# A transformer block on one core: the sums of squares of all eight tiles on VectorE, and one matmul with ones in place of three (two)

## The chip, the cores and the metric

The kernel runs on one core of a Trainium2 chip. TensorE multiplies, VectorE (DVE), ScalarE (ACT) and GpSimd (POOL) do the elementwise work, SyncE (SP) issues the loads of the weights. The metric is the device time of one execution in microseconds, the median of the runs shown.

## The reference, cut to what matters

Four layers of a first model and one layer of a second work on x of 256 tokens by 1024 channels, in float32. Each layer is an attention or a mixer, a projection back to 1024, and a gated feed-forward block. Ahead of each of these stands an RMS norm over the 1024 channels of a token:

```
def rmsnorm(x, g):
    xf = x.astype(jnp.float32)
    y = xf * lax.rsqrt(jnp.mean(xf * xf, axis=-1, keepdims=True) + EPS)
    return (y * g.astype(jnp.float32)).astype(x.dtype)
...
        x = x + m @ w_o[layer]
        h = rmsnorm(x, ffn_norm[layer])
        x = x + conv_gated_ffn(h, ffn_w_up[layer], ffn_conv_w[layer], ffn_conv_b[layer], ffn_w_down[layer])
```

The change touches only how the sum of xf * xf over the channels is made.

## The kernel before

x lies in SBUF transposed: eight tiles of 128 channels (partitions) by 256 tokens. A sum over channels is so a sum of the eight squared tiles, and then a sum over the 128 partitions, which a matmul with a 128x128 matrix of ones does (`statistic`); its result stands on every partition, in the bank `ov`.

The weights come in chunks of 1 MB or more through a ring of three buffers. Each chunk is split in two parts that TensorE can take fast: ACT rounds it to `w_hi` (L322), DVE makes the rest `w_lo` (L805). The activations are split the same way, `h_hi` by ACT and `h_lo` by DVE or POOL. A product takes three matmuls: hi by hi, lo by hi, hi by lo. All order is written by hand: each engine has one program, a loop over the stages (attention "da", "sb", "sw", "mix"; projection "wo"; "up"; "down"; "gate"), and semaphores tie them. A stage takes its chunks in turn.

There are 13 norms, listed in `SUMS`: "x" at the start, "wo0" to "wo3", "down0" to "down3", "final", "wo4", "res_a" and "down4". For each, ACT squares the tiles into `sq` (`squares`, L352), DVE adds them into `acc` (`add_squares`, L842) and TensorE sums over the partitions (`statistic`, L1601 for `acc`, L1605 for squares that are not in `acc`). For "down" norms each tile is squared by itself, and DVE has added seven; for the others tiles 0 to 5 are squared two by two and added by DVE, and tiles 6 and 7 go to TensorE as they are. Then `rms` on ACT (L365 Ln, L366 Exp) makes `rstd` out of the sum, DVE's `normalise` makes the normed tiles (`hf`, the rows `tmp<-x,par,rstd` of L854), ACT rounds them (`h_hi`, L376), and DVE (even tiles, L850) and POOL (odd tiles, L1345) make `h_lo`.

The first chunk of the stage behind "wo0" to "wo3", "down0" to "down2", "final" and "res_a" does not wait for the norm. It multiplies x times its gain, without rstd ("raw" tiles: `raw_high` on ACT L380, `raw_low` on DVE L863 and on POOL L1357 and L1360), and its result is scaled by rstd afterwards (`scaled_first`, L870, or L1235). In `first_outputs` TensorE walks over the eight tiles k; for each tile it does six matmuls (L1529 with `h_hi`, L1538 with `h_lo`), and at one k it does the statistic of the norm:

```
if raw is not None and k == (1 if raw[0:2] in ("wo", "do") else 5):
    statistic(raw)
```

The second chunk of the stage needs the normed tiles, and the third chunk is the first that is a plain product (L1484 to L1486). DVE's order behind a projection is: adding the last tiles to x, raw tiles 6 and 7, the `w_lo` of the stage's second chunk, `normalise`, the `w_lo` of its third chunk. ACT's is: `rms`, the `w_hi` of the third chunk (L322), `split_h` (L376). Behind a down projection DVE's is: raw tile 7, `normalise`, the scaling of the first chunk's result, the `w_lo` of three chunks.

For "x", "down3", "wo4" and "down4" the statistic stands alone, and TensorE has nothing of the next stage before the norm.

Of the kernel before, what the change touches and what calls it, by code (L numbers as in the profile page):

```python
# [33 lines left out]
S = 256  # L34
QB = 128
D = 1024
DT = D // P
# [47 lines left out]
def build(nc, xT, w_std, w_down, w_gate, params, consts, lam, onehot, tables, pT, out):  # L85
    ctx = ExitStack()
    with ctx:
# [10 lines left out]
        x = sb("x", [P, DT, S])  # L98
# [151 lines left out]
        SUMS = {}  # L250
        added = parts = 0
        for name, singles in ([("x", False)]
                              + [(f"{k}{l}", k == "down") for l in range(4) for k in ("wo", "down")]
                              + [("final", False), ("wo4", False), ("res_a", False), ("down4", True)]):
            SUMS[name] = (added, parts, len(SUMS))
            added, parts = added + (7 if singles else 5), parts + (8 if singles else 5)

        def is_single(name):
            return name[0:4] == "down"
# [537 lines left out]
        def _(dve):  # L797
# [25 lines left out]
            def add_squares(name, j):  # L823

                n = sum_part(name, j)[2]
                total = acc[:, 0:S]
                dve.wait_ge(sq_ready, SUMS[name][1] + j + 1)
                if is_single(name):
                    terms = [(total, sq[:, n, 0:S])]
                    before = j  # L830
                else:
                    terms = [(total, sq[:, n, 0:S]), (total, sq[:, n, S:2 * S])]
                    before = max(2 * j - 1, 0)
                    if j == 0:
                        terms = [(sq[:, n, 0:S], sq[:, n, S:2 * S])]
                for k, (a, b) in enumerate(terms):
                    if SUMS[name][0] + before + k:
                        dve.wait_ge(acc_done, SUMS[name][0] + before + k)
                    if j == 0 and is_single(name):
                        dve.tensor_copy(total, b).then_inc(acc_done, 1)  # L840
                    else:
                        dve.tensor_tensor(total, a, b, ALU.add).then_inc(acc_done, 1)  # L842
# [133 lines left out]
            dve.memset(odd[:, 7:8], EPS).then_inc(dve_step, 1)  # L976
            steps[0] += 1
            wait_step()
            for j in range(3):
                add_squares("x", j)  # L980
            split_lo(0, 0, SIZES[0])

# [39 lines left out]
            def sum_behind(name, k):  # L1022

                for t in (k - 1, k) if k == DT - 1 else (k - 1,):
                    if t >= 0 and raw_engine(app, t):
                        raw_low(app, t)
                if k % 2 and k > 1:
                    add_squares(name, k // 2 - 1)

            half = s_half = d_half = ffn = app = 0  # L1030
            layer = 0
# [2 lines left out]
            for kind, c0, n in STAGES:  # L1034
# [127 lines left out]
                elif kind == "wo":  # L1162
# [26 lines left out]
                    added_to_x(4)  # L1189
                    if layer < 4:  # L1190
                        raw_low(app, 6)
                        raw_low(app, 7)
                        next_split(c0, 2)
                        normalise(app, SUMS[name][2])
                        next_split(c0, 3)
                    else:
                        dve.wait_ge(rstd_done, SUMS[name][2] + 1)
                        def behind(k):
                            sum_behind("res_a", k)
                            if k == DT // 2:  # L1200
                                next_split(c0, 2)

                        add_normed("mix_post", x_ready, behind)
                        normalise(app, SUMS["res_a"][2])
                        next_split(c0, 3)
# [69 lines left out]
                elif kind == "down":  # L1275
                    name = f"down{layer}"
                    for k in range(DT):
                        if layer < 4:
                            dve.wait_ge(used, c0 + k + 1)
                            dve.tensor_tensor(x[:, k, :], pj[slot_of(c0, k)][:, 0:S], x[:, k, :], ALU.add)\  # L1280
                               .then_inc(x_main, 1)
                            dve.wait_ge(x_main, layer * DT + k + 1)
                            dve.tensor_tensor(x[:, k, :], pj[slot_of(c0, k)][:, S:2 * S], x[:, k, :], ALU.add)\  # L1283
                               .then_inc(bank_free, 1)
                        if k < DT - 1:
                            add_squares(name, k)
                        if layer < 3 and raw_engine(app, k):
                            raw_low(app, k)
                        if k < DT - 1:
                            next_split(c0, k)  # L1290
# [186 lines left out]
        def _(pe):  # L1477
# [38 lines left out]
            def first_outputs(app, sums, shared=True, raw=None):  # L1516

                for k in range(DT):  # L1520
                    if raw is None:
                        pe.wait_ge(h_hi_done, app * DT + k + 1)
                    else:
                        pe.wait_ge(raw_hi, raw_count(app, k))
                    for n, (dst, operands) in enumerate(sums):
                        (wh, wl), (xh, xl), swap = operands(k)
                        for w in (wh, wl):
                            a, b = (xh, w) if swap else (w, xh)
                            pe.matmul(dst, a, b, start=k == 0 and w is wh and (n == 0 or not shared),  # L1529
                                      stop=False, skip_group_check=shared)  # L1530
                    if raw is None:
                        pe.wait_ge(h_lo_odd if k % 2 else h_lo_even, app * (DT // 2) + k // 2 + 1)
                    else:
                        pe.wait_ge(raw_lo[raw_engine(app, k)], raw_lo_count(app, k))
                    for n, (dst, operands) in enumerate(sums):
                        (wh, wl), (xh, xl), swap = operands(k)
                        a, b = (xl, wh) if swap else (wh, xl)
                        done = pe.matmul(dst, a, b, start=False, stop=k == DT - 1, skip_group_check=shared)  # L1538
                    if raw is not None and k < DT - 1:
                        done.then_inc(raw_used, 1)  # L1540
                    if raw is not None and k == (1 if raw[0:2] in ("wo", "do") else 5):
                        statistic(raw)
                return done

# [50 lines left out]

            def statistic(name):

                singles = is_single(name)
                added, parts, _ = SUMS[name]
                pe.wait_ge(acc_done, added + (7 if singles else 5))  # L1600
                pe.matmul(ov[:, 0:S], ones, acc[:, 0:S], start=True, stop=False)  # L1601
                for j in ((7,) if singles else (3, 4)):
                    _, (a, b), n = sum_part(name, j)
                    pe.wait_ge(sq_ready, parts + j + 1)
                    done = pe.matmul(ov[:, 0:S], ones, sq[:, n, a:b], start=False, stop=j in (7, 4))  # L1605
                done.then_inc(stat_done, 1)

            def scores(s_half, q_tile, k_tile):
# [529 lines left out]
```

## Time and profile before

| | |
|---|---|
| median of 3 runs | 1587.36 us (1586.63 to 1589.05) |
| the profiled execution | 1588.9 us, its span from the first to the last instruction 1587.3 us |
| mean granted TensorE clock | 0.986 of full speed |
| busy share of the span | PE 96%, weight loads 91%, DVE 66%, ACT 54%, POOL 20% |
| loads of weights | 1 MB (most), landing 4.9 us after their issue |

The profile lists busy time by engine and the chain of work that ended last. An instruction's row gives its start, its duration, its engine and line, what it writes and reads, and in brackets how long the engine sat idle before it and which instruction released it. TensorE's rows overlap: a matmul of 256 columns lasts 0.28 us, and the next starts 0.12 us later at full clock. A matmul in float32 (the ones by `acc` or `sq`) appears as two rows, since it is done in two passes.

### The profile page before, as it was taken

The numbers are of one execution on the slowest core, as the hardware profiler recorded it, in microseconds if no ns is written. First come the engines' busy times: TensorE is split into PE (matmuls) and PEld (weight loads), VectorE is DVE, ScalarE is ACT, GpSimd is POOL, SyncE is SP. The second block draws the span as 40 slices with busy tenths as digits, with TensorE's granted clock in tenths as the row PEclk, the third lists the DMA queues.
The fourth block names the chain that finished last, engine by engine and source line by source line (L and its number), as shares of the span: only waits on it lengthen the run. The fifth ranks groups of instructions, "written<-read, shape, count | busy, mean of one in ns | idle before, by whom it ended". The sixth has DMA issues, their size and how long they took to land.

```text
span 1587.3 us, 31012 instructions
## 1 busy us (share of the span) xinstructions
PE 1527.1 (96%) x11566; PEld 1438.0 (91%) x11566; DVE 1050.1 (66%) x1671; ACT 862.6 (54%) x1347; POOL 316.1 (20%) x474
## 2 busy tenths in 40 slices
PE   6999999999999999988999999999999898899998
PEld 5988999899989998878999889899998797899997
DVE  5667877563378775667877566688776655866545
ACT  4766555455565554555656356665554455544533
POOL 2102212212222112212222220032110361212100
PEclk9999999999999999999999999999999898899999
DMA  7543656353335564442656455436564353355550
GB/s 258 160 168 110 210 185 241 136 180 112 127 110 209 185 243 135 152 160 80 212 185 214 169 178 162 153 119 205 182 241 153 104 189 107 133 185 195 190 205 27
DMA packets 36666, 264.65 MB, mean 167 GB/s; under 512 B 4767, under 2 KB 4826, under 8 KB 7792
## 3 DMA queue, kind: packets, MB, share of 16 engines
q1 hardware_dynamic: 33552, 255.59, 46.4%
q0 software_dynamic: 3040, 8.05, 2.0%
q8 instruction: 49, 0.80, 0.2%
q14 instruction: 25, 0.20, 0.0%
HBM read 262.50 MB, written 1.12 MB: 166 GB/s over the span
## 4 chain that ended last, share of the span: by engine, by line
PE 81%; DVE 11%; ACT 5%; issue 2%; DMA 1%; SPq 0%; POOL 0%; ACTq 0%; DVEq 0%
PE bank L1484 20%; PE bank L1485 19%; PE bank L1486 19%; PE bank L1495 10%; PE bank L1494 6%; DVE w_lo L805 3%; DVE tmp L854 2%; PE bank L1529 1%; ACT tmp L396 1%; ACT w_hi L322 1%; DVE acc L842 1%; PE bank L1637 1%; DVE tmp L886 1%; DVE h_lo L850 1%; DVE w_lo L814 1%
## 5 line engine op out<-in xcount | busy, mean ns | idle before, releaser
L805 DVE TENSOR_TENSOR w_lo<-w_raw,w_hi 128x2048 fp32r<-128x2048 f32 (+2 forms) x220 | 543.2, 2472 | 222.9 <-ACT w_hi L322 222.8
L1484 PE MATMUL bank<-h_hi,w_hi 128*128 128x256 f32 x2032 | 579.3, 285 | 2.1 <-DVE w_lo L805 2.1
L1485 PE MATMUL bank<-h_lo,w_hi 128*128 128x256 f32 x2032 | 574.9, 283 | 0.0
L1486 PE MATMUL bank<-h_hi,w_lo 128*128 128x256 f32 x2032 | 574.9, 283 | 0.0
L322 ACT CAST w_hi<-w_raw 128x2048 fp32r<-128x2048 f32 (+2 forms) x220 | 445.3, 2025 | 5.6 <-DMA w_raw<-w_std 2.8
L1484 PEld LDWEIGHTS bank<-h_hi,w_hi 128*128 128x128 f32 x2032 | 389.5, 192 | 8.0 <-issue 4.1
L1485 PEld LDWEIGHTS bank<-h_lo,w_hi 128*128 128x128 f32 x2032 | 389.7, 192 | 0.1
L1486 PEld LDWEIGHTS bank<-h_hi,w_lo 128*128 128x128 f32 x2032 | 389.6, 192 | 0.0
L1495 PE MATMUL bank<-act_both,w_hi 128*128 128x512 f32 (+1 forms) x704 | 248.7, 394 | 0.0
L734 ACT ACTIVATE tmp<-bank,par 128x256 f32<-128x256 f32 x181 | 93.4, 561 | 227.5 <-PE bank L1486 226.9
L1243 DVE SCALAR_TENSOR_TENSOR tmp<-bank,par,tmp 128x255 f32<-128x255 f32 (+1 forms) x362 | 155.4, 477 | 84.8 <-ACT tmp L734 82.1
L1494 PE MATMUL bank<-act_both,w_lo 128*128 128x256 f32 (+1 forms) x704 | 203.6, 289 | 0.0
L1484 PE MATMUL bank<-act_both,w_hi 128*128 128x256 f32 x516 | 150.5, 292 | 6.9 <-DVE act_both L958 5.2
L1495 PEld LDWEIGHTS bank<-act_both,w_hi 128*128 128x128 f32 (+1 forms) x704 | 131.9, 187 | 27.7
L1485 PE MATMUL bank<-act_both,w_hi 128*128 128x256 f32 x516 | 146.4, 284 | 0.0
L1486 PE MATMUL bank<-act_both,w_lo 128*128 128x256 f32 x516 | 146.4, 284 | 0.0
L1494 PEld LDWEIGHTS bank<-act_both,w_lo 128*128 128x128 f32 (+1 forms) x704 | 132.7, 189 | 15.0 <-issue 15.0
L1455 POOL CAST act_both<-tmp 128x256 f32 x110 | 43.6, 397 | 480.9 <-DVE tmp L1260 370.9
L352 ACT ACTIVATE sq<-x 128x256 f32<-128x256 f32 (+1 forms) x67 | 31.9, 479 | 161.9 <-DVE x L1283 149.6
L1484 PEld LDWEIGHTS bank<-act_both,w_hi 128*128 128x128 f32 x516 | 99.3, 192 | 13.2 <-DVE act_both L958 7.1
L1357 POOL TENSOR_SCALAR proj<-x,par 128x256 f32<-128x256 f32 x35 | 44.4, 1270 | 331.1 <-ACT h_hi L380 331.1
L1529 PE MATMUL bank<-h_hi,w_hi 128*128 128x256 f32 x320 | 92.8, 309 | 13.8 <-ACT h_hi L376 8.3
(165 smaller groups left out, 2130.5 us busy)
## 6 DMA issues: line engine op xcount, KB each, us to landing
w_raw<-w_std SPq DMA_DIRECT2D x181, 1024.0 KB, 4.9
w_raw<-w_down SPq DMA_DIRECT2D x40, 1408.0 KB, 6.2
act_both<-vec_dram POOLq DMA_DIRECT2D x56, 128.0 KB, 3.4
w_raw<-w_gate SPq DMA_DIRECT2D x4, 1280.0 KB, 5.4
x<-xT SPq DMA_DIRECT2D x2, 512.0 KB, 4.9
out<-x SPq DMA_DIRECT2D x4, 256.0 KB, 2.2
par<-params SPq DMA_DIRECT2D x1, 499.0 KB, 9.4
cst<-consts SPq DMA_DIRECT2D x1, 256.0 KB, 5.8
```

Of the source, the lines that this page charges most:

```text
L322: act.copy(w_hi[:, slot, 0:width], w_raw[:, slot, 0:width]).then_inc(hi_ready, 1)
L734: act.activation(to[:, slot, :], source, ACT.Identity, bias=col(3), scale=col(2)).then_inc(conv_init, 1)
L805: dve.tensor_tensor(w_lo[:, slot, 0:width], w_raw[:, slot, 0:width], w_hi[:, slot, 0:width].bitcast(F32), ALU.subtract).then_inc(lo_ready, 1)
L1243: return dve.scalar_tensor_tensor(to[:, slot, lag:S], source(v)[:, 0:S - lag], par[:, bass.ds(at + (4 * v + 2 - lag), 1)], to[:, slot, lag:S],
L1357: pool.tensor_scalar(proj[:, k % 4, :], x[:, k, :], gain_of(app, k), None, ALU.mult)\
L1455: pool.tensor_copy(act_hi[:, bass.ds(j, 1), :].squeeze(1) if not isinstance(j, int) else act_hi[rows, j, :], cval[rows, slot, :]).then_inc ...
L1484: pe.matmul(dst, wh, xh, start=first, stop=False, skip_group_check=shared)
L1485: pe.matmul(dst, wh, xl, start=False, stop=False, skip_group_check=shared)
L1486: done = pe.matmul(dst, wl, xh, start=False, stop=last, skip_group_check=shared)
L1494: pe.matmul(bank[:, 0:S], wl, xh, start=start and k == 0, stop=False, skip_group_check=True)
L1495: done = pe.matmul(bank[:, :], wh, pair, start=False, stop=stop and k == len(weights) - 1, skip_group_check=True)
L1529: pe.matmul(dst, a, b, start=k == 0 and w is wh and (n == 0 or not shared), stop=False, skip_group_check=shared)
```

## The change

DVE now adds all eight squared tiles into `acc`, and `statistic` is one matmul of ones by `acc`. `add_squares` has two more calls for the norms that squared pairs, and one more for the down norms. In `first_outputs` the statistic now stands behind tile 3 where a down norm is made, and behind tile 6 for all others.

```diff
             SUMS[name] = (added, parts, len(SUMS))
-            added, parts = added + (7 if singles else 5), parts + (8 if singles else 5)
+            added, parts = added + (8 if singles else 7), parts + (8 if singles else 5)
...
                     if j == 0:
                         terms = [(sq[:, n, 0:S], sq[:, n, S:2 * S])]
+                    elif j >= 3:
+                        terms = [(total, sq[:, n, (j - 3) * S:(j - 2) * S])]
+                        before = j + 2
...
-            for j in range(3):
+            for j in range(5):
                 add_squares("x", j)
...
                 if k % 2 and k > 1:
                     add_squares(name, k // 2 - 1)
+                if k == DT - 1:
+                    add_squares(name, 3)
+                    add_squares(name, 4)
...
                     if layer < 4:
                         raw_low(app, 6)
+                        add_squares(name, 3)
                         raw_low(app, 7)
+                        add_squares(name, 4)
                         next_split(c0, 2)
                         normalise(app, SUMS[name][2])
                         next_split(c0, 3)
                     else:
+                        add_squares(name, 3)
+                        add_squares(name, 4)
                         dve.wait_ge(rstd_done, SUMS[name][2] + 1)
...
-                        if k < DT - 1:
-                            add_squares(name, k)
+                        add_squares(name, k)
...
-                    if raw is not None and k == (1 if raw[0:2] in ("wo", "do") else 5):
+                    if raw is not None and k == {"d": 3, "w": 6}.get(raw[0], 6):
                         statistic(raw)
...
-                singles = is_single(name)
-                added, parts, _ = SUMS[name]
-                pe.wait_ge(acc_done, added + (7 if singles else 5))
-                pe.matmul(ov[:, 0:S], ones, acc[:, 0:S], start=True, stop=False)
-                for j in ((7,) if singles else (3, 4)):
-                    _, (a, b), n = sum_part(name, j)
-                    pe.wait_ge(sq_ready, parts + j + 1)
-                    done = pe.matmul(ov[:, 0:S], ones, sq[:, n, a:b], start=False, stop=j in (7, 4))
+                if name == "x":
+                    pe.wait_ge(consts_in, 16)
+                pe.wait_ge(acc_done, SUMS[name][0] + (8 if is_single(name) else 7))
+                done = pe.matmul(ov[:, 0:S], ones, acc[:, 0:S], start=True, stop=True)
                 done.then_inc(stat_done, 1)
```

The lines of the changed kernel are numbered three and more higher. TensorE at the head of the first up stage (norm "wo0"), before; the rows are of tiles 1 and 2:

```order
L1529 MATMUL bank<-h_hi,w_lo 128x256
L1538 MATMUL bank<-h_lo,w_hi 128x256 [waits raw_lo1]
L1538 MATMUL bank<-h_lo,w_hi 128x256
L1601 MATMUL bank<-acc,cst 128x256 [waits acc_done]
L1605 MATMUL bank<-sq,cst 128x256 [waits sq_ready] x2
L1529 MATMUL bank<-h_hi,w_hi 128x256 [waits raw_hi]
L1529 MATMUL bank<-h_hi,w_lo 128x256
```

And of the change, the rows of tiles 6 and 7 and the first of the second chunk:

```order
L1547 MATMUL bank<-h_lo,w_hi 128x256 [waits raw_lo1]
L1547 MATMUL bank<-h_lo,w_hi 128x256
L1610 MATMUL bank<-acc,cst 128x256 [waits acc_done]
L1538 MATMUL bank<-h_hi,w_hi 128x256 [waits raw_hi]
L1538 MATMUL bank<-h_hi,w_lo 128x256
L1538 MATMUL bank<-h_hi,w_hi 128x256
L1538 MATMUL bank<-h_hi,w_lo 128x256
L1547 MATMUL bank<-h_lo,w_hi 128x256 [waits raw_lo1]
L1547 MATMUL bank<-h_lo,w_hi 128x256
L1538 MATMUL bank<-h_hi,w_hi 128x256 [waits h_hi_done,bank_free,lo_ready]
```

Two of three matmuls with ones are gone, and between the remaining one and the second chunk stand six matmuls (tile 7), where there were 36 (tiles 2 to 7).

VectorE at the end of the first projection ("wo0"), before, from the last two adds to x on:

```order
L1176 TENSOR_TENSOR x<-bank,x 128x256 [waits tile6_done]
L1176 TENSOR_TENSOR x<-bank,x 128x256 [waits used]
L863 SCALAR_TENSOR_TENSOR h_lo<-x,par,h_hi 128x256 [waits raw_hi] x2
L805 TENSOR_TENSOR w_lo<-w_raw,w_hi 128x2048 [waits hi_ready]
L854 SCALAR_TENSOR_TENSOR tmp<-x,par,rstd 128x256 [waits rstd_done]
L854 SCALAR_TENSOR_TENSOR tmp<-x,par,rstd 128x256 x3
L850 TENSOR_TENSOR h_lo<-tmp,h_hi 128x256 [waits h_hi_done]
```

And of the change:

```order
L1182 TENSOR_TENSOR x<-bank,x 128x256 [waits tile6_done]
L1182 TENSOR_TENSOR x<-bank,x 128x256 [waits used]
L866 SCALAR_TENSOR_TENSOR h_lo<-x,par,h_hi 128x256 [waits raw_hi]
L845 TENSOR_TENSOR acc<-acc,sq 128x256 [waits acc_done,sq_ready]
L866 SCALAR_TENSOR_TENSOR h_lo<-x,par,h_hi 128x256 [waits raw_hi]
L845 TENSOR_TENSOR acc<-acc,sq 128x256 [waits acc_done,sq_ready]
L805 TENSOR_TENSOR w_lo<-w_raw,w_hi 128x2048 [waits hi_ready]
L857 SCALAR_TENSOR_TENSOR tmp<-x,par,rstd 128x256 [waits rstd_done]
```

Two adds stand between the raw tiles and ahead of the `w_lo` of the second chunk.

VectorE at the end of the first down projection ("down0"), before:

```order
L1280 TENSOR_TENSOR x<-bank,x 128x256 [waits used]
L1283 TENSOR_TENSOR x<-bank,x 128x256 [waits x_main]
L863 SCALAR_TENSOR_TENSOR h_lo<-x,par,h_hi 128x256 [waits raw_hi]
L854 SCALAR_TENSOR_TENSOR tmp<-x,par,rstd 128x256 [waits rstd_done]
L854 SCALAR_TENSOR_TENSOR tmp<-x,par,rstd 128x256 x3
```

And of the change:

```order
L1290 TENSOR_TENSOR x<-bank,x 128x256 [waits used]
L1293 TENSOR_TENSOR x<-bank,x 128x256 [waits x_main]
L845 TENSOR_TENSOR acc<-acc,sq 128x256 [waits acc_done,sq_ready]
L866 SCALAR_TENSOR_TENSOR h_lo<-x,par,h_hi 128x256 [waits raw_hi]
L857 SCALAR_TENSOR_TENSOR tmp<-x,par,rstd 128x256 [waits rstd_done]
```

The eighth add stands ahead of the raw tile 7. The orders of ACT, POOL and SP are the same as before.

## Rows read from the trace of the kernel before

**Rows 1.** The page: busy time and share by engine, with the instructions' count.

```profile
PE 1527.1 (96%) x11566; PEld 1438.0 (91%) x11566; DVE 1050.1 (66%) x1671; ACT 862.6 (54%) x1347; POOL 316.1 (20%) x474
```

**Rows 2.** The page: shares of the chain that ended last.

```profile
PE 81%; DVE 11%; ACT 5%; issue 2%; DMA 1%; SPq 0%; POOL 0%; ACTq 0%; DVEq 0%
```

**Rows 3.** The lines of the statistic: duration min/median/max in ns, first and last start.

```profile
L1601 PE MATMUL bank<-acc,cst x26: 377/379/792, 8.7 to 1549.9; 128*128 128x256 f32 x26
L1605 PE MATMUL bank<-sq,cst x42: 378/379/634, 9.6 to 1550.6; 128*128 128x256 f32 x42
```

**Rows 4.** Timeline around norm "wo0", TensorE: start, duration, row, idle before and releaser.

```profile
137.89 0.70 PE L1601 MATMUL bank<-acc,cst 128*128 128x256 f32 x2 [0.90 <-DVE acc L842]
139.29 1.40 PE L1605 MATMUL bank<-sq,cst 128*128 128x256 f32 x4 [0.70 <-ACT sq L352]
140.34 0.47 PE L1529 MATMUL bank<-h_hi,w_hi 128*128 128x256 f32 x1
...
151.82 0.39 PE L1484 MATMUL bank<-h_hi,w_hi 128*128 128x256 f32 x1 [0.43 <-DVE w_lo L805]
```

**Rows 5.** Timeline around norm "wo0", VectorE.

```profile
139.66 0.48 DVE L863 SCALAR_TENSOR_TENSOR h_lo<-x,par,h_hi 128x256 fp32r<-128x256 f32 x1 [0.55 <-ACT h_hi L380]
140.37 0.48 DVE L863 SCALAR_TENSOR_TENSOR h_lo<-x,par,h_hi 128x256 fp32r<-128x256 f32 x1 [0.22 <-ACT h_hi L380]
140.77 2.29 DVE L805 TENSOR_TENSOR w_lo<-w_raw,w_hi 128x2048 fp32r<-128x2048 f32 x1
142.97 1.67 DVE L854 SCALAR_TENSOR_TENSOR tmp<-x,par,rstd 128x256 f32<-128x256 f32 x4
144.56 0.41 DVE L850 TENSOR_TENSOR h_lo<-tmp,h_hi 128x256 fp32r<-128x256 f32 x1
...
148.94 2.82 DVE L805 TENSOR_TENSOR w_lo<-w_raw,w_hi 128x2048 fp32r<-128x2048 f32 x1
```

**Rows 6.** Timeline around norm "wo0", ScalarE, and GpSimd's last raw tile.

```profile
140.73 0.47 ACT L365 ACTIVATE rstd<-bank,odd 128x256 f32<-128x256 f32 x1 [0.39 <-PE bank L1605]
141.56 1.90 ACT L322 CAST w_hi<-w_raw 128x2048 fp32r<-128x2048 f32 x1
...
138.71 0.72 POOL L1360 TENSOR_TENSOR h_lo<-proj,h_hi 128x256 fp32r<-128x256 f32 x1
```

**Rows 7.** Timeline around norm "down0", TensorE.

```profile
330.30 0.59 PE L1601 MATMUL bank<-acc,cst 128*128 128x256 f32 x2
330.73 0.59 PE L1605 MATMUL bank<-sq,cst 128*128 128x256 f32 x2
...
341.89 0.38 PE L1484 MATMUL bank<-w_hi,h_hi 128*128 128x256 f32 x1 [0.50 <-DVE w_lo L805]
```

**Rows 8.** Timeline around norm "down0", ScalarE and VectorE.

```profile
331.36 0.48 ACT L365 ACTIVATE rstd<-bank,odd 128x256 f32<-128x256 f32 x1 [0.74 <-PE bank L1605]
...
332.32 1.67 DVE L854 SCALAR_TENSOR_TENSOR tmp<-x,par,rstd 128x256 f32<-128x256 f32 x4 [1.18 <-ACT rstd L366]
...
339.56 6.70 DVE L805 TENSOR_TENSOR w_lo<-w_raw,w_hi 128x2048 fp32r<-128x2048 f32 x3
```

**Rows 9.** Timelines around norms "down3", "final" and "res_a".

```profile
1241.22 0.70 PE L1605 MATMUL bank<-sq,cst 128*128 128x256 f32 x2 [0.80 <-ACT sq L352]
...
1251.43 0.88 DVE L842 TENSOR_TENSOR acc<-acc,sq 128x256 f32<-128x256 f32 x2
...
1357.67 1.22 PE L1601 MATMUL bank<-acc,cst 128*128 128x256 f32 x2 [2.04 <-DVE acc L842]
...
1360.64 0.47 ACT L365 ACTIVATE rstd<-bank,odd 128x256 f32<-128x256 f32 x1 [4.03 <-PE bank L1605]
```

**Rows 10.** An idle time of TensorE; stretches behind it: busy times, clock, DMA share, GB/s.

```profile
1257.13 0.36 PE L1529 MATMUL bank<-h_hi,w_hi 128*128 128x256 f32 x1 [1.77 <-ACT h_hi L376]
...
1258.00:1260.00 2.00, 2.00 (x12) 2.00 (x11) 2.00 (x5) 0.81 (x2) 1.20 (x3) 0.52 0.00 0
1260.00:1262.00 2.00, 2.00 (x13) 2.00 (x13) 2.00 (x6) 1.49 (x3) 1.20 (x2) 0.62 0.03 8
```

## The prediction

> **What bounds the kernel now.** Read the busy shares first: TensorE is busy for 96% of the span and VectorE for 66% [rows 1], so at first sight whatever leaves TensorE is gain. The chain that ended last says nearly the same, 81% TensorE [rows 2], but it gives 16% to VectorE and ScalarE together, and one must find where. The third view is the pair of lines that the change edits: 26 rows for 13 matmuls of ones by `acc` and 42 rows for 21 matmuls of ones by `sq` [rows 3]. The fourth is the timeline around one norm of each kind, one engine at a time. There the reader is to look for the row in which TensorE stops last, and at who released it. Behind "wo0" that is the first matmul of the third chunk, 151.82, which sat idle 0.43 us for VectorE's `w_lo` [rows 4]; behind "down0" it is the same matmul of the next stage, 341.89, idle 0.50 us for `w_lo` [rows 7]. So the work just behind a norm is not paced by TensorE. It is paced by VectorE, which does raw tile, `w_lo`, `normalise`, `w_lo` without a gap from 140.37 on [rows 5], and behind "down0" by the chain statistic, rstd, `normalise`, `w_lo` [rows 8]. The norms repeat to within 0.05 us: four like "wo0" (wo0 to wo3) and three like "down0" (down0 to down2).
>
> **The change, part by part.** A float32 matmul of ones by 256 columns takes 0.43 us of TensorE at full clock (from 330.30 to 330.73 [rows 7]); its result is there 0.59 us after its start when TensorE was running, 0.70 when it had been idle [rows 4, 7]. The change removes 21 of them, 9.0 us of TensorE. An add on VectorE lasts 0.42 us and a second one, which waits for the first, starts 0.46 later (0.88 for two [rows 9]); between other work an add takes the queue 0.34. The change adds 21 of them. Neither sum is a time yet: what counts is when rstd comes and when the third chunk's `w_lo` is ready.
>
> The Trainium skill ("VectorE: DVE Perf Modes", section "The DRAIN you can't avoid") says that a semaphore between two VectorE operations costs nothing extra. By its rule the dependent adds would stand 0.34 us apart and not 0.46, and the sum below would be 0.5 us less; the trace does not agree with it for these short adds.
>
> *wo0 to wo3.* Before, TensorE did tiles 0 and 1, waited 0.90 us for the sum, waited again 0.70 us for tile squares, and went on with tile 2 at 140.34 [rows 4]. Now it does tiles 2 to 6 meanwhile. Tile 4 has to wait for POOL's `h_lo`, done at 138.71 + 0.72 = 139.43 [rows 6]; with 0.1 us for the semaphore and 0.24 for the two matmuls left of it, tiles 5 and 6 (0.72 each) end at about 141.2. VectorE: raw tile 6 at 139.66; the add of tile 6 fits ahead of raw tile 7 (its square is long done, and VectorE sat idle 0.22 us there), which so starts at 140.40; the add of tile 7 starts at 140.80 and ends at 141.22. So the matmul with ones starts at about 141.3, both inputs arriving together, and ends at 142.0; Ln starts there, not at 140.73 [rows 6], 1.25 us later. What is late next? ACT's `w_hi` cast, 0.83 behind Ln, starts at 142.8 and takes 1.9, and `h_hi` of tile 0, 0.4 us more, is done at about 145.15. VectorE's `w_lo` starts at 141.15 in place of 140.77, `normalise` at 143.35 (rstd is there at 142.95, no wait), its four rows end the queue at 144.95, and then `h_lo` of tile 0 waits for `h_hi` until 145.2; before, it started at 144.56 [rows 5]. From there VectorE is 0.64 us late, and the second `w_lo` (148.94, 2.82 us [rows 5]) with it. The third chunk starts 0.64 us late. All later work hangs on it, so it is not given back.
>
> TensorE is done with tile 7 at about 142.6 and can start the second chunk at 145.25: 2.65 us idle in one piece. Behind 1.77 us of idle time at 1257.13 the granted clock was 0.52 of full in the two microseconds from 1258 and 0.62 in the next two [rows 10]: 1.92 + 1.52 = 3.4 us at 1.2 GHz in place of 2.4. If the clock falls like that in the second chunk too, TensorE does in 3.4 us what takes 1.7 at full clock and loses 1.7; the chunk's own waits for VectorE's tiles swallow a good half, and the third chunk would start some 0.9 us late in all. Bounds: 0.64 (the clock stays) and 2.0 (it stays low for 6 us of the chunk). I take 0.9, since the idle time is longer than in the row. 4 x 0.9 = 3.6.
>
> *down0 to down2.* Before, the statistic stood behind tile 1 at 330.30, two matmuls, result at 331.32, Ln at 331.36 [rows 7, 8]. Now tiles 2 and 3 come first, 2 x 0.72, so the matmul starts at 331.74 and Ln at 331.74 + 0.59 + 0.04 = 332.37, 1.0 us later. The eighth add is free: it fills VectorE's wait for raw tile 7. But `normalise` sat idle 1.18 us for rstd at 332.32 [rows 8]: nothing covers the delay there, and `h_hi`, `h_lo`, the scaling and the `w_lo` at 339.56 all come 1.0 us later. The matmul at 341.89, which had waited for that `w_lo` 0.50 us, comes at 342.9. TensorE saved 0.43 us and waits longer for it. 3 x 1.0 = 3.0. Bounds: 0.5 (if 0.50 us of it were slack; it is not, it is idle time on the same side) and 1.4 (TensorE's tiles alone).
>
> *down3, wo4, down4.* The statistic is alone, and the square of the last tile comes last (TensorE idle 0.80 us for it at 1241.22 [rows 9]). Before, one matmul followed it; now an add, 0.42 + 0.03, and the matmul. +0.45 each, 1.35. Lower bound 0.3, where two matmuls had followed.
>
> *final and res_a.* The two adds stand behind the last raw tile. "final": 2 x 0.46 on VectorE against two matmuls of about 0.43 and a shorter end: +0.05. "res_a": the clock was low there, three matmuls lasted from 1357.67 to Ln at 1360.64, 2.97 us [rows 9]; now 0.92 for the adds, 1.22 for one matmul and 0.1 of semaphores: 2.2, so -0.75. The matmuls of tile 6 run in the wait.
>
> *x.* Ln waits there for ACT's first cast, which waits for the first weights' DMA: nothing. If that cover were gone it would cost 0.1.
>
> Sum: 3.6 + 3.0 + 1.35 + 0.05 - 0.75 = +7.2 us. The profiled execution took 1588.9 us (span 1587.3), so a like one would take 1596.1 (span 1594.5); the median of the runs shown lies 1.5 us lower than the profiled one, 1587.36, which gives **1594.6 us**, 0.45% more.
>
> **The rivals.**
>
> *TensorE is the bound after all (faster).* If the second and third chunk did not wait for VectorE, the 21 matmuls would be gain. Behind "wo" TensorE would lose the piece from 136.99 (137.89 less its idle time) to 140.34, less one matmul and POOL's wait, some 2.5 us, x 4; behind "down" 0.43 x 3; the rest +0.6: -10.7 us, 1576.7. For it speaks the 96% [rows 1]; against it the two `w_lo` waits of TensorE [rows 4, 7]. It decides from the point at which `w_lo` of the third chunk comes before TensorE ends the second; it came 0.4 to 0.5 us after.
>
> The Trainium skill ("Perfetto Trace Analysis", section "Identifying the Most-Contended Engine") would have one optimize the engine with the highest occupancy first, for TensorE by its weight loads, 91% here. By that rule taking work from TensorE and giving it to VectorE, at 66%, is the right trade, and the time would be near this rival's; the idle rows behind each norm do not agree.
>
> *Slack further down takes it back (no change).* The delays of wo and down could be absorbed in the stages behind, if TensorE there waited for something that does not hang on these chains, such as a DMA. Then only the lone norms remain: +0.65, 1588.0; with half absorbed 1591. For it: ScalarE's casts do now and then wait for a load. Against it: DMA has 1% of the chain [rows 2].
>
> *The clock falls deep behind wo (slower still).* With the low clock over 6 us of each second chunk, 2.0 us in place of 0.9: +11.6, 1599.0.
>
> **How the numbers follow.** The likeliest is as summed, chance 0.66, own range 1592 to 1597.5. TensorE bound: 0.13. Absorbed: 0.13. Deep clock: 0.08. A measurement of this kernel tells a change of over 0.2% (3.2 us) from none. So faster 0.13, same 0.14, slower 0.73. The range of 8 in 10 leaves out the faster rival and the far end of the clock one: 1588 to 1599.
>
> **What would show it.** In the changed kernel's trace: one matmul with ones per norm; behind "wo0" Ln about 1.25 us later against its stage, TensorE idle 2 to 3 us in front of the second chunk for `h_hi`, `h_lo` of tile 0 waiting on ScalarE, a granted clock below 1 in the second chunk, and the third chunk 0.6 to 1.1 us late. Behind "down0" Ln and the third chunk each 1.0 us late. The prediction is wrong if the third chunk starts when it did or earlier, or if Ln is not late: then I have misread which input of the statistic comes last.

## The result, and the profile after

The changed kernel takes 1594.43 us (median of 5 runs, 1594.13 to 1597.78), the kernel before 1587.36 us beside it (5 runs, 1586.63 to 1589.1). The ratio is 1.0046, 95% interval 1.0035 to 1.0058: it is slower by about half a per cent. 1594.6 was forecast.

The page of the changed kernel, busy shares and then the shares of the chain that ended last:

```profile
PE 1520.8 (95%) x11524; PEld 1433.4 (90%) x11524; DVE 1058.6 (66%) x1692; ACT 861.2 (54%) x1347; POOL 314.3 (20%) x474
PE 82%; DVE 10%; ACT 4%; issue 3%; DMA 1%; SPq 0%; POOL 0%; DVEq 0%; ACTq 0%
```

Against [rows 1] TensorE lost 42 rows (21 float32 matmuls, two rows each) and 6.3 us of busy time, VectorE gained 21 instructions and 8.5 us, and the span grew from 1587.3 to 1592.5. The engine with the highest share got less to do and the kernel got slower. Nothing on the page says why; the stages behind the norms do. All rows below are read against an offset, the time of a row in this trace less the time of the same row in the trace of before: the changed kernel reaches "wo0" 1.16 us early (GpSimd's last raw tile starts at 137.55, against 138.71 [rows 6]). That comes from the start of the program and has nothing to do with the change; the first experiment and the last show why.

The timeline of TensorE at "wo0", changed kernel (start, duration, row, idle time before and its releaser):

```profile
140.11 0.70 PE L1610 MATMUL bank<-acc,cst 128*128 128x256 f32 x2
140.46 0.47 PE L1538 MATMUL bank<-h_hi,w_hi 128*128 128x256 f32 x1
...
144.01 0.36 PE L1538 MATMUL bank<-h_hi,w_hi 128*128 128x256 f32 x1 [2.49 <-ACT h_hi L376]
...
151.25 0.39 PE L1493 MATMUL bank<-h_hi,w_hi 128*128 128x256 f32 x1 [0.43 <-DVE w_lo L805]
```

ScalarE and then VectorE in the same place:

```profile
140.85 0.47 ACT L365 ACTIVATE rstd<-bank,odd 128x256 f32<-128x256 f32 x1 [1.67 <-PE bank L1610]
141.35 0.42 ACT L366 ACTIVATE rstd<-rstd 128x256 f32<-128x256 f32 x1
141.68 1.88 ACT L322 CAST w_hi<-w_raw 128x2048 fp32r<-128x2048 f32 x1
143.47 1.32 ACT L376 CAST h_hi<-tmp 128x256 fp32r<-128x256 f32 x4
```

```profile
138.91 0.42 DVE L845 TENSOR_TENSOR acc<-acc,sq 128x256 f32<-128x256 f32 x1
139.24 0.48 DVE L866 SCALAR_TENSOR_TENSOR h_lo<-x,par,h_hi 128x256 fp32r<-128x256 f32 x1
139.64 0.42 DVE L845 TENSOR_TENSOR acc<-acc,sq 128x256 f32<-128x256 f32 x1
139.97 2.28 DVE L805 TENSOR_TENSOR w_lo<-w_raw,w_hi 128x2048 fp32r<-128x2048 f32 x1
142.18 1.67 DVE L857 SCALAR_TENSOR_TENSOR tmp<-x,par,rstd 128x256 f32<-128x256 f32 x4
143.90 0.43 DVE L853 TENSOR_TENSOR h_lo<-tmp,h_hi 128x256 fp32r<-128x256 f32 x1
...
148.37 2.83 DVE L805 TENSOR_TENSOR w_lo<-w_raw,w_hi 128x2048 fp32r<-128x2048 f32 x1
```

The reader is to see that the two waits of [rows 4] at the norm (0.90 and 0.70 us) are gone, and that one of 2.49 us stands a chunk later instead. Ln is at 140.85 against 140.73 [rows 6]: with the 1.16 us, 1.28 late. The second `w_lo` is at 148.37 against 148.94 [rows 5], 0.59 late; the third chunk at 151.25 against 151.82 [rows 4], 0.59 late, with the same wait for `w_lo` in front of it, 0.43 us. What TensorE no longer does at the norm it waits for later.

The same at "down0", TensorE, then ScalarE and VectorE:

```profile
331.17 0.59 PE L1610 MATMUL bank<-acc,cst 128*128 128x256 f32 x2
...
342.32 0.39 PE L1493 MATMUL bank<-w_hi,h_hi 128*128 128x256 f32 x1 [0.55 <-DVE w_lo L805]
```

```profile
331.80 0.47 ACT L365 ACTIVATE rstd<-bank,odd 128x256 f32<-128x256 f32 x1 [1.75 <-PE bank L1610]
...
332.76 1.67 DVE L857 SCALAR_TENSOR_TENSOR tmp<-x,par,rstd 128x256 f32<-128x256 f32 x4 [2.19 <-ACT rstd L366]
...
339.99 4.48 DVE L805 TENSOR_TENSOR w_lo<-w_raw,w_hi 128x2048 fp32r<-128x2048 f32 x2
```

The offset ahead of this norm is -0.58 us. Ln (331.36 before), `normalise` (332.32), `w_lo` (339.56 [rows 8]) and the third chunk (341.89 [rows 7]) all come 0.43 to 0.44 later than before, so 1.0 us late each: a delay that passes through undiminished.

To see where the 5.2 us between the two spans came up, the starts of ScalarE's 230 weight casts in both traces are set side by side, after minus before, in order. The offset moves in few places:

| place | offset moves by, us | forecast |
|---|---|---|
| start to the end of the first layer's attention | -1.19 | 0 |
| wo0, wo1, wo2, wo3 | +0.61, +0.57, +0.54, +0.60 | +0.9 each |
| down0, down1, down2 | +1.02, +1.01, +1.00 | +1.0 each |
| down3 and final | +0.64 | +0.50 |
| wo4 | +0.34 | +0.45 |
| res_a | -0.84 | -0.75 |
| down4 | +0.44 | +0.45 |
| small steps elsewhere (766 us +0.09, 984 to 1006 us +0.19, 1316 us +0.21) | +0.49 in all | 0 |
| sum | +5.2 | +7.2 |

### The profile page after: what moved, and what is told of

The parts are those of the page before. It is cut to its first block, busy times and chain, and to the rows that moved or that the text cites. A ratio compares the mean times of both kernels' runs of the same rounds, so it can differ in the third digit from the quotient of the medians.

```text
span 1592.5 us, 30970 instructions
## 1 busy us (share of the span) xinstructions
PE 1520.8 (95%) x11524; PEld 1433.4 (90%) x11524; DVE 1058.6 (66%) x1692; ACT 861.2 (54%) x1347; POOL 314.3 (20%) x474
## 4 chain that ended last, share of the span: by engine, by line
PE 82%; DVE 10%; ACT 4%; issue 3%; DMA 1%; SPq 0%; POOL 0%; DVEq 0%; ACTq 0%
PE bank L1493 20%; PE bank L1494 19%; PE bank L1495 19%; PE bank L1504 10%; PE bank L1503 6%; PE bank L1538 2%; DVE w_lo L805 2%; DVE tmp L857 1%; DVE acc L845 1%; ACT tmp L396 1%; PE bank L1547 1%; PE bank L1642 1%; ACT w_hi L322 1%; DVE tmp L889 1%; DVE w_lo L814 1%
```

## The experiments

The offsets below are found in the same way, against the first trace of the kernel before.

**The kernel before once more.** The code is unchanged.

> The kernel before, unchanged, for a second profile of it. The profiles so far differ by 5.2 us of span while the medians differ by 7.1. If 1.2 us of that are the phase of TensorE's clock in the first 25 us, this profile will show the span either near 1587.3 with the low clock until about 22 us, or near 1585.5 to 1586 with the low clock until about 20 us. If instead the first 25 us are the same and the span differs, the difference sits at another place.

It took 1588.72 us (one run), span 1587.1. Its offset is -0.74 us at the end of the first attention, -0.68 at 755 us, -0.50 from 767 us and -0.20 from 1316 us on. What differs at the start is the granted clock. Stretches of 4 us of the first trace of the kernel before (busy times with their counts, then the clock, DMA share, GB/s):

```profile
14.00:18.00 4.00, 1.70 (x7) 1.64 (x8) 4.00 (x7) 1.59 (x4) 1.37 (x2) 0.71 0.94 324
18.00:22.00 4.00, 4.00 (x21) 4.00 (x21) 3.26 (x7) 2.59 (x5) 2.26 (x3) 0.50 0.40 170
```

and of this run:

```profile
14.00:18.00 4.00, 2.01 (x8) 1.95 (x9) 4.00 (x8) 1.76 (x5) 1.67 (x2) 1.00 0.88 326
18.00:22.00 4.00, 4.00 (x23) 4.00 (x23) 2.96 (x6) 2.73 (x5) 1.96 (x3) 1.00 0.34 141
```

Between 18 and 22 us TensorE ran at 1.2 GHz (0.50) in the one and at 2.4 GHz in the other, same code. In the changed kernel that stretch is at 1.00 as well. So the -1.19 us of the table is such a chance: the kernel of the last experiment, which is the kernel before up to that point, has -1.16 at the same place. The steps of the table at 766 us (+0.09) and 1316 us (+0.21) are of the same kind, since the unchanged code has +0.18 and +0.30 there. At 1316 us other traces of this case move by -1.1 or +1.9, so one pair of traces is good to 1 to 2 us in all, while the own step of each wo and down0 to down2 norm repeats to about 0.05 as long as TensorE is not what paces it.

**The adds and the one matmul, at the old place.** VectorE adds all eight tiles, TensorE does one matmul, but behind tile 1 (wo, down) and tile 5 (others), as before.

```diff
-                    if raw is not None and k == {"d": 3, "w": 6}.get(raw[0], 6):
+                    if raw is not None and k == (1 if raw[0:2] in ("wo", "do") else 5):
```

> The change without its move: VectorE adds all eight tiles, one matmul with ones, but behind tile 1 (wo, down) and tile 5 (final, res_a) as before. My theory (rstd and VectorE's queue set the time): behind down Ln comes only 0.1 us later than before, behind wo the third chunk still 0.6 us late, the lone norms as in the change: 1587.4 + 0.3 + 2.3 + 0.7 = 1590.5 to 1591.5, some 3 us under the change. Theory TensorE is the bound: TensorE then waits until 141.3 behind wo with its tiles 2 to 7 still to do, 1.4 us later than before, 1593 or more, not better than the change.

1597.56 us (5 runs, 1596.71 to 1598.48), ratio 1.0065 [1.0052, 1.0079]: slower than the whole change. My expectation missed by 6 us; the rival written beside it, TensorE as the bound with 1593 or more, is what came. Down norms cost 0.10 us each, as expected. A wo norm costs 1.5 to 2.6 us (wo0 1.5, wo1 2.6, wo2 2.4, wo3 1.5) in place of 0.6. TensorE at "wo0":

```profile
140.77 0.77 PE L1610 MATMUL bank<-acc,cst 128*128 128x256 f32 x2 [4.28 <-DVE acc L845]
141.12 0.63 PE L1538 MATMUL bank<-h_hi,w_hi 128*128 128x256 f32 x1
141.56 0.41 PE L1538 MATMUL bank<-h_hi,w_lo 128*128 128x256 f32 x1
...
152.89 0.28 PE L1493 MATMUL bank<-h_hi,w_hi 128*128 128x256 f32 x1
```

and the stretches behind it:

```profile
141.00:143.00 2.00, 2.00 (x10) 1.92 (x10) 2.00 (x2) 1.39 (x3) 0.00 (x0) 0.57 0.05 12
143.00:145.00 2.00, 2.00 (x13) 2.00 (x12) 1.87 (x6) 2.00 (x4) 0.01 (x1) 0.58 0.38 74
```

The two waits of before became one of 4.28 us, all 36 matmuls of tiles 2 to 7 are still to be done behind it, the first 15 of them at 1.2 GHz (0.41 us each), and the third chunk at 152.89 starts without a wait: here TensorE really is the bound. What I had left out is how late the sum is when VectorE does all of it: 140.77 is, with this run's offset of -0.49, 2.0 us after the last wait of before ended (139.29 [rows 4]).

What makes TensorE the bound is its clock. The `w_lo` that the third chunk needs starts at 149.11 and is done at 151.94, only 0.66 us late in its stage (148.94 [rows 5] before), so the other 0.8 us of wo0's 1.5 are TensorE's. Stretches of 8 us behind wo0 to wo3, this run:

```profile
141.00:149.00 8.00, 8.00 (x54) 7.92 (x54) 7.87 (x13) 5.54 (x11) 2.45 (x3) 0.79 0.38 134
459.00:467.00 8.00, 7.38 (x38) 7.21 (x39) 7.51 (x13) 4.78 (x10) 1.92 (x3) 0.59 0.37 133
746.00:754.00 8.00, 7.19 (x38) 7.01 (x39) 7.51 (x13) 4.72 (x9) 1.72 (x3) 0.61 0.37 131
1059.00:1067.00 8.00, 8.00 (x55) 7.97 (x54) 7.95 (x14) 5.54 (x11) 2.57 (x4) 0.79 0.36 131
```

A mean clock of 0.79 over 8 us means 3.4 us at 1.2 GHz, in which TensorE loses 1.7 us of work; 0.59 means 6.6 us and 3.3. The two norms with 0.79 cost 1.5 us each, the two with 0.59 and 0.61 cost 2.6 and 2.4. At full clock throughout, by this estimate, wo0's third chunk could start at 151.2, before its `w_lo` is done, and the norm would cost the 0.66 of VectorE, as I had expected. So most of the 6 us by which the expectation missed is the price of the clock, which it left out.

**The old three (two) matmuls, at the new place.** The other half alone.

```diff
-                    if raw is not None and k == (1 if raw[0:2] in ("wo", "do") else 5):
+                    if raw is not None and k == {"d": 3, "w": 6}.get(raw[0], 6):
```

> The move alone: three (two) matmuls with ones as before, but behind tile 3 (down) and tile 6 (wo, final, res_a). My theory: behind down Ln 1.44 us late, times 3 = 4.3; behind wo the three matmuls end at 142.7 of the old time, h_hi of tile 0 comes at 145.8 and VectorE is 1.2 us late, times 4 = 5; final 0.5: about 1597 to 1598, slower than the change. Theory TensorE is the bound: filling TensorE's waits behind wo gains and the move costs nothing behind down: 1581 to 1587.

1596.67 us (5 runs, 1595.48 to 1597.51), ratio 1.0055 [1.0042, 1.0069]. Each down norm costs 1.44 us, exactly the two tiles of 0.72 that now stand ahead of the matmuls; each wo norm 1.32 to 1.36. At "wo0" the three matmuls (140.79 to 142.25) put Ln at 142.29. This is as expected. With the run before it gives a square for a wo norm: old 0, adds alone 1.5 to 2.6, place alone 1.3, both 0.6. The halves don't add, and the adds alone are dear through the low clock: with the new place TensorE has its tiles 2 to 6 to do meanwhile and waits 2.49 us in place of 4.28. For a down norm: 0, 0.10, 1.44, 1.01.

**The change, with the statistic of down norms at tile 1.**

```diff
-                    if raw is not None and k == {"d": 3, "w": 6}.get(raw[0], 6):
+                    if raw is not None and k == {"d": 1, "w": 6}.get(raw[0], 6):
```

> The change with only the down norms' statistic put back behind tile 1. My theory: three times 1.0 us comes back less 0.1 each, so 2.7 us under the change: 1591.7. Theory TensorE is the bound: the same as the change, 1594.4, since TensorE does the same work without any wait of its own there.

1592.38 us (7 runs, 1591.04 to 1593.16), ratio 1.0029 [1.0017, 1.0040]. The steps of the down norms fell from 1.0 to 0.1 each and those of wo stayed at 0.56 to 0.60, so the 3.0 us of the prediction's second term are the place of the matmul behind tile 3 and nothing else. TensorE and ScalarE at "down0":

```profile
330.95 0.70 PE L1610 MATMUL bank<-acc,cst 128*128 128x256 f32 x2 [0.27 <-DVE acc L845]
331.69 0.47 ACT L365 ACTIVATE rstd<-bank,odd 128x256 f32<-128x256 f32 x1 [0.85 <-PE bank L1610]
```

TensorE does wait there, 0.27 us, which is why one may think a later place is better; that wait is not on the path, and rstd is.

**The idle time filled.** To the changed kernel five more float32 matmuls of ones by a constant are added behind the first chunk of the four wo stages. Their result goes to an unused bank; the output is unchanged.

```diff
+                if raw is not None and raw[0:2] == "wo":
+                    for _ in range(5):
+                        pe.matmul(banks[6][:, 0:S], ones, cst[:, 0:S], start=True, stop=True)
```

> The change, with five matmuls of constants into an unused bank behind the first chunk of the up stages of wo0 to wo3, 2.15 us of work in TensorE's 2.49 us of idle time, so that the clock does not fall. Theory A (VectorE's queue sets the third chunk's start; the low clock in the second chunk is hidden): the same time as the change within 0.3 us, 1594.4, and the wo offsets stay at 0.57 us each. Theory B (my prediction's term: the low clock costs part of 0.9 us): 1 to 1.5 us less than the change, about 1593.

1595.64 us (5 runs, 1594.91 to 1596.43), ratio 1.0044 [1.0030, 1.0058], the same as the change's. The second chunks of wo1 to wo3 in the changed kernel:

```profile
459.00:468.00 9.00, 6.51 (x40) 6.28 (x39) 8.94 (x14) 5.53 (x11) 3.18 (x4) 0.81 0.33 117
745.00:754.00 9.00, 6.51 (x39) 6.17 (x38) 8.94 (x14) 5.53 (x11) 3.17 (x4) 0.81 0.35 117
1056.00:1066.00 10.00, 7.51 (x48) 7.23 (x48) 9.94 (x15) 5.53 (x11) 3.19 (x4) 0.83 0.29 105
```

and with the five matmuls:

```profile
459.00:468.00 9.00, 8.26 (x56) 7.26 (x54) 8.94 (x16) 5.54 (x11) 2.45 (x3) 1.00 0.33 117
745.00:754.00 9.00, 8.28 (x56) 7.35 (x55) 8.95 (x16) 5.49 (x12) 2.45 (x3) 1.00 0.34 118
1056.00:1066.00 10.00, 9.28 (x64) 8.27 (x63) 9.94 (x17) 5.59 (x12) 3.20 (x4) 1.00 0.31 105
```

TensorE's clock is back at 2.4 GHz throughout these stretches, VectorE's busy time (the third number: 8.94, 8.95, 9.94) has not moved by more than 0.01 us, and neither have the steps (0.60, 0.62, 0.61 and 0.58). With the low clock the third chunk of wo1 starts at 470.20 without a wait, with the full clock at 471.02 behind a wait of 0.43; less their offsets (+1.01 and +1.93) that is 469.19 and 469.09. The low clock costs 0.1 us there, and 0.2 at wo2 by the same reckoning; the casts behind show none of it.

**VectorE's first `w_lo` ahead of the scaling** (kernel before, down norms). I asked whether the order of VectorE behind a norm could give back what the change costs.

```diff
+                    postponed_splits()
...
-                    postponed_splits()
```

> The kernel before, with VectorE's next weight split ahead of the scaling of the first chunk's result (behind the down norms and final). If the third chunk waits for that split as the rows say (0.50 us), TensorE goes on 0.5 to 0.6 us earlier at three or four places: 1585.3 to 1586. If the scaling is what the attention stage needs first, it gives that back: 1587.3 or more.

1586.90 us (11 runs, 1585.29 to 1588.99) against 1588.79 (27 runs, 1585.73 to 1590.99), ratio 0.9990 [0.9981, 0.9999]: at the edge of what can be told, and not for my reason. VectorE and ScalarE behind "down0":

```profile
339.11 2.83 DVE L805 TENSOR_TENSOR w_lo<-w_raw,w_hi 128x2048 fp32r<-128x2048 f32 x1
341.86 0.74 DVE L870 SCALAR_TENSOR_TENSOR proj<-bank,rstd 128x256 f32<-128x256 f32 x2
342.64 1.91 ACT L322 CAST w_hi<-w_raw 128x2048 fp32r<-128x2048 f32 x1 [3.68 <-DVE proj L870]
```

`w_lo` comes earlier, but ScalarE's next cast waits 3.68 us for the scaling, where it waited 0.93 before, and nearly all of the gain is given back within the stage: each down norm's step is -0.1 us. The profiled gain, 2.5 us, comes up at two places that the edit does not touch: -1.15 at 1316 us, where the traces of two other kernels of this case, which have no such edit, move by -1.14, and -1.36 at res_a, where TensorE's clock was at full in this trace and low in the trace of before (see the last run).

**The last raw tiles of wo on GpSimd** (kernel before). VectorE's raw tiles 6 and 7 go to GpSimd, which has been idle since 139.43.

```diff
-            return int(k >= 6 or (app % 2 and k % 2))
+            return int(k % 2 and k < 6) if app % 2 else int(k >= 6)
...
-                        raw_low(app, 6)
-                        raw_low(app, 7)
+                        for k in (6, 7):
+                            if raw_engine(app, k):
+                                raw_low(app, k)
```

> The kernel before, with the raw tiles 6 and 7 behind wo0 to wo3 on GpSimd in place of VectorE. If VectorE's queue is the bound there, its split and normalise come 1.3 us earlier and h_lo of tile 0 then waits for ScalarE: the third chunk 0.6 us earlier, times 4, so 1584.9. If GpSimd is late with tile 7 (it stood 3.05 us on one product beside VectorE's split), the second chunk starts later and nothing or less is gained: 1587 to 1589.

1587.92 us (11 runs, 1587.41 to 1593.08), ratio 1.0003 [0.9994, 1.0012]: nothing. VectorE and GpSimd at "wo0", and the last row of the path:

```profile
138.30 2.54 DVE L805 TENSOR_TENSOR w_lo<-w_raw,w_hi 128x2048 fp32r<-128x2048 f32 x1
138.99 2.64 POOL L1358 TENSOR_SCALAR proj<-x,par 128x256 f32<-128x256 f32 x1 [0.30 <-ACT h_hi L380]
140.95 2.41 DVE L854 SCALAR_TENSOR_TENSOR tmp<-x,par,rstd 128x256 f32<-128x256 f32 x4
...
148.25 2.82 DVE L805 TENSOR_TENSOR w_lo<-w_raw,w_hi 128x2048 fp32r<-128x2048 f32 x1
```

VectorE starts `w_lo` 1.7 us earlier in its stage, and then both engines slow down beside each other: `w_lo` 2.54 for 2.29, `normalise`'s four rows 2.41 for 1.67, GpSimd's product, beside `w_lo`, 2.64 for 1.09. GpSimd's second product, at 142.43 beside `normalise`, took 1.09 as usual. The second `w_lo` is at 148.25; the offset there is -0.74, so 148.20 would have been no change.

**Both of them together.**

> Both edits on the kernel before. If they act at different norms, as the rows say, the two differences add: about 1583 to 1584 if each does what the theory of VectorE's queue says, 1587 or more if neither.

1587.16 us (11 runs, 1586.55 to 1589.92), ratio 0.9997 [0.9988, 1.0006]. Neither adds to the other.

**The change for res_a alone**, in the kernel before: the one norm at which the table shows a gain.

```diff
-            added, parts = added + (7 if singles else 5), parts + (8 if singles else 5)
+            added, parts = added + (7 if singles or name == "res_a" else 5), parts + (8 if singles else 5)
...
+                if name == "res_a" and k == DT - 1:
+                    add_squares(name, 3)
+                    add_squares(name, 4)
...
+                if name == "res_a":
+                    pe.wait_ge(acc_done, added + 7)
+                    pe.matmul(ov[:, 0:S], ones, acc[:, 0:S], start=True, stop=True).then_inc(stat_done, 1)
+                    return
```

> The kernel before, changed for one norm alone, res_a: VectorE adds all eight squared tiles and TensorE does one matmul with ones, behind tile 6 in place of tile 5. All other norms keep their two or three matmuls. My account of the change says that this is the one norm at which it gains, 0.84 us, since the statistic there waits for VectorE's last square anyway and TensorE runs at its lower clock when it comes. Under it the time is 0.8 us below the kernel before, about 0.05%, and the Ln behind res_a comes 0.8 us earlier against its own stage. The rival is that the 0.84 us in the profile of the change was a chance of the clock's phase there: then Ln of res_a comes where it did, and the time is that of before, plus or minus 0.5. The time alone can hardly tell the two apart (one execution differs from the next by more), so the rows of TensorE and ScalarE at this norm decide. If both a gain of 0.8 there and a time that is not lower show up, the gain is given back in the stages behind.

1587.80 us (11 runs, 1587.10 to 1589.85) against 1588.78 (15 runs, 1585.97 to 1589.90), ratio 0.9996 [0.9987, 1.0005]. VectorE, TensorE and ScalarE at the norm:

```profile
1357.65 1.94 DVE L845 TENSOR_TENSOR acc<-acc,sq 128x256 f32<-128x256 f32 x4
1359.63 1.22 PE L1608 MATMUL bank<-acc,cst 128*128 128x256 f32 x2 [2.05 <-DVE acc L845]
1360.89 0.47 ACT L365 ACTIVATE rstd<-bank,odd 128x256 f32<-128x256 f32 x1 [3.37 <-PE bank L1608]
```

From the first of the last adds to Ln it is 3.24 us (1360.89 less 1357.65); before it was 3.90 (1360.64 [rows 9] less 1356.74, where those adds start). The offset moves by -0.66 there. TensorE ran at 1.2 GHz in both: the matmul with ones takes 1.22 us here and in [rows 9].

But the gain belongs to the low clock. In the three experiments just above, this norm is as in the kernel before and its matmuls with ones ran at the full clock. The adds and Ln, first in the run with the raw tiles on GpSimd (the old three matmuls), then in the change with the statistic of down norms at tile 1 (the one matmul, at full clock too):

```profile
1356.74 0.88 DVE L842 TENSOR_TENSOR acc<-acc,sq 128x256 f32<-128x256 f32 x2
1359.28 0.47 ACT L365 ACTIVATE rstd<-bank,odd 128x256 f32<-128x256 f32 x1 [2.67 <-PE bank L1606]
```

```profile
1360.61 1.94 DVE L845 TENSOR_TENSOR acc<-acc,sq 128x256 f32<-128x256 f32 x4
1363.34 0.47 ACT L365 ACTIVATE rstd<-bank,odd 128x256 f32<-128x256 f32 x1 [2.85 <-PE bank L1610]
```

That is 2.54 us the old way and 2.73 with the adds: at full clock the change loses 0.19 us here. "final", which does the same work and had the full clock in both first traces, agrees: 2.53 (1251.43 [rows 9] to 1253.96) before, 2.72 (1256.31 to 1259.03) after. The clock alone is worth more than the change: in those three runs the offset moves by -1.36 at res_a with the code unchanged.

The time of the whole kernel shows none of this: this trace came 1.9 us late out of 1295 to 1323 us, ahead of the norm, and the interval spans 2.9 us.

## Why the prediction was right, by its steps

**TensorE does not pace the work behind a norm: right.** The third chunk of "wo0" and "down0" waits for VectorE's `w_lo` before and after, by 0.43 us at "wo0" and by 0.50 and 0.55 us at "down0". (At wo1 to wo3 of the changed kernel it starts 0.1 to 0.2 us after `w_lo` is done, through the low clock.) The rival in which TensorE is the bound (1576.7) is out: 21 matmuls left it and every wo and down norm got slower. It was not far off, though: the run with the old place shows that with 4.28 us of waiting in one piece, and the low clock behind it, TensorE becomes the bound, and that costs more time still. The Trainium skill ("Perfetto Trace Analysis", section "Identifying the Most-Contended Engine") would optimize the engine with the highest occupancy first, TensorE's judged by its weight loads. Here these went from 91% to 90%, VectorE stayed at 66%, and the time went up by 0.46%: taking work off the busiest engine did not pay by itself.

**wo0 to wo3: mechanism right, the size too large.** Of 0.9 us a norm, 0.64 was the queue of VectorE and measured 0.59 at "wo0" (the second `w_lo`). Ln was forecast 1.25 late and is 1.28; the wait for `h_hi` was forecast at 2.65 us and is 2.49. The rest, 0.26, was for the clock, and that was wrong. The clock did fall, to 0.81 to 0.83 over the second chunks of wo1 to wo3, yet those steps (0.57, 0.54, 0.60) are no larger than that of wo0 (0.61), where it stayed at 1.00, and filling the gap made none smaller. The sentence that failed is "the chunk's own waits for VectorE's tiles swallow a good half": they swallow all but 0.1 to 0.2 us, and the start of the third chunk is set by VectorE, whose busy time did not move with TensorE's clock (8.94 us in both traces). Four times 0.33 too much is 1.3 us. The term was not empty in kind, though: behind the longer wait of the run with the old place the clock did cost 0.8 us and more a norm.

**down0 to down2: right to 0.02 us.** Shown from both sides: the matmul behind tile 1 takes it to 0.1, two matmuls behind tile 3 make it 1.44.

**down3, final, wo4, down4: right.** +0.64, +0.34 and +0.44 against 0.50, 0.45 and 0.45; "final" was put at 0.05 and is 0.19. **res_a: right, in part by luck.** -0.84 against -0.75. The forecast took over the low clock of the trace before, and the trace of the change had the low clock for most of this norm as well. Adds to Ln take 3.90 us before, 3.24 with the change at low clock throughout and 3.06 in its first trace, so 0.66 of the 0.84 is the change and 0.18 the clock; at full clock in both the term would have been +0.19. **x: right.** Ln follows ScalarE's own cast before it (10.86 + 1.90, Ln at 12.66) without a gap, with the sum ready by then: the matmul with ones was done at 10.69.

**The adds.** Beside other work an add takes 0.33 us of the queue (138.91 to 139.24, 139.64 to 139.97), as forecast with 0.34. Four that wait for one another take 1.93 to 1.94 us, so they start 0.50 apart, not 0.46. The Trainium skill ("VectorE: DVE Perf Modes", section "The DRAIN you can't avoid") has it, from a row of eight copies, that a semaphore between VectorE operations costs nothing extra. Here the dependent adds are 0.17 us further apart, but the adds between other work wait for semaphores too, ones that had long come. So the prediction went too far where it set this against the page: what costs is that the awaited result comes from the operation just before.

**The total.** By the table the change itself is +6.1 us (5.2 plus the 1.19 that came from the start, less 0.3 for the steps at 766 and 1316 us, which the unchanged code has too), of 7.2 forecast: 1.3 too much for the clock at wo, and 0.2 between 984 and 1006 us that was not foreseen. The medians differ by 7.07 us, with an interval of 5.6 to 9.2 by the ratio, which holds 6.1 and 7.2. That 1594.6 met 1594.43 so closely is so in part luck: the sum was 1.1 us too high, and a median of few runs moves by as much.

The rival of slack further down is out as well: once the stage behind a norm is over, the offset does not go back. What stays open is the 0.2 us between 984 and 1006 us: it stands in the traces of all four kernels in which VectorE adds everything (0.19 to 0.21) and in neither the unchanged kernel (0.04) nor the one with the place alone (0.00), so it belongs to the adds, by a way that no run here shows.

## What to carry to other kernels

Before moving work off the busiest engine, find the row in which it last waits ahead of the stage's first free-running piece. If another engine releases it there, the work taken away turns into a longer wait, and what counts is when the shared result (here rstd) is ready. A reduction's last step belongs as early as its input allows: two tiles later cost 1.0 to 1.4 us each time, with no wait of TensorE at the sum itself to show for it.

Test the halves of a change apart. Here the adds alone cost 1.5 to 2.6 us at a wo norm, the later place alone 1.3, both together 0.6. And before a gain at one place is believed, look at the granted clock there in both traces: at res_a it decided between -0.66 and +0.19.

## What the runs showed of the hardware

The granted clock of one and the same code differs from run to run in fixed places: between 18 and 22 us it was 0.50 in one trace and 1.00 in another, with the offset 0.74 us apart by the end of that stage, and the kernel before ran from 1585.7 to 1591.0 us in 27 runs. Behind a wait of 2.49 us it stayed at 1.00 in one of four equal stages and fell in three, at a cost of 0.2 us at most, since VectorE paced them; behind 4.28 us it fell in all four and cost 0.8 us or more each. At 1.2 GHz three float32 matmuls and their sum take 2.97 us ([rows 9]), at 2.4 GHz 1.60 (1357.68 to 1359.28, in the run with the raw tiles on GpSimd). And VectorE and GpSimd can slow each other when both run elementwise rows at once: by 1.1 times (`w_lo`, 2.54 for 2.29), 1.4 times (`normalise`, 2.41 for 1.67) and 2.4 times (GpSimd's product, 2.64 for 1.09), though one product beside `normalise` kept its 1.09.
